# Paired units of a split-precision matmul kernel: the high and the low products in alternation instead of one run after the other

## What is computed

```python
def reference(x, ...):
    x = first_block(x, ...)      # norm, stick-breaking attention (16 heads), w_o, squared-ReLU MLP of width 8192
    return second_block(x, ...)  # 16 meta tokens ahead; w_in (12288 wide), pooling and conv branches, gates,
                                 # conv_out_w, w_o, gated MLP of width 5632 (w_gate_up, w_down), final norm
```

## Time and profile before

| | |
|---|---|
| median of 3 runs | 2644.3 us |
| the profiled execution, its own time | 2644.36 us |
| its span, first to last instruction | 2642.6 us |
| outside of the span | 1.8 us |
| TensorE matmul busy | 2620.2 us (99%), 16669 matmuls |
| VectorE / ScalarE / GpSimd busy | 63% / 46% / 15% |
| DMA | 54.7% of the 16 engines' time, 183 GB/s |
| highs (L1154) | 5248, of 512 columns |
| lows (L1160) | 5248, of 256 columns |

### The profile page before, as it was taken

The page is one execution under the profiler, slowest core; times in us unless marked ns, Lnnn a source line. Parts: engine busy times, 40 slices in busy tenths (PEclk is TensorE's granted clock), DMA queues, the critical chain, the costliest instruction groups (busy, mean ns, idle before and its releaser), DMA issues.

```text
span 2642.6 us, 41760 instructions
## 1 busy us (share of the span) xinstructions
PE 2620.2 (99%) x16669; PEld 2375.9 (90%) x16669; DVE 1657.6 (63%) x1279; ACT 1204.7 (46%) x1161; POOL 396.9 (15%) x180
## 2 busy tenths in 40 slices
PE   8999999999999999999999999999999999999998
PEld 8999999888888888899899988888888888888898
DVE  5566666656556556898754776566756555655555
ACT  5455554444444444533533344444444444444444
POOL 2122222100001001442200530011211001100110
PEclk9999999999999999999999999999999999999999
DMA  7554455555555555554555555555555555555552
GB/s 233 186 174 149 157 176 185 184 189 190 191 188 184 186 190 191 175 181 166 204 183 185 181 190 185 184 189 191 185 186 187 191 191 188 183 186 190 191 190 97
DMA packets 242948, 484.25 MB, mean 183 GB/s; under 512 B 7600, under 2 KB 7808, under 8 KB 242816
## 3 DMA queue, kind: packets, MB, share of 16 engines
q1 hardware_dynamic: 242800, 482.60, 54.7%
q10 hardware_dynamic: 32, 0.01, 0.0%
HBM read 480.49 MB, written 2.10 MB: 183 GB/s over the span
## 4 chain that ended last, share of the span: by engine, by line
PE 94%; issue 3%; POOL 1%; DVE 1%; ACT 1%; DMA 0%; ACTq 0%; POOLq 0%; DVEq 0%
PE ps L1154 44%; PE ps L1160 22%; PE ps L1172 15%; PE ps L1178 7%; PE ps L1142 2%; PE ps L1148 1%; POOL S L982 1%; POOL U L1023 0%; POOL a_buf L977 0%; DVE wlo L680 0%; PE ps L1121 0%; PE ps L1122 0%; PE ps L1120 0%; PE ps L1227 0%; PE ps L1204 0%
## 5 line engine op out<-in xcount | busy, mean ns | idle before, releaser
L680 DVE TENSOR_TENSOR wlo<-raw,whi 128x1024 fp32r<-128x1024 f32 x912 | 1263.2, 1398 | 929.1 <-ACT whi L511 928.6
L511 ACT ACTIVATE whi<-raw 128x1024 fp32r<-128x1024 f32 x912 | 964.6, 1060 | 1324.6 <-PE ps L1160 990.5
L1154 PE MATMUL ps<-b_buf,whi 128*128 128x512 f32 x2688 | 673.3, 392 | 0.0
L1154 PE MATMUL ps<-a_buf,whi 128*128 128x512 f32 x2560 | 645.7, 394 | 0.0
L1154 PEld LDWEIGHTS ps<-b_buf,whi 128*128 128x128 f32 x2688 | 483.5, 189 | 86.5
L1154 PEld LDWEIGHTS ps<-a_buf,whi 128*128 128x128 f32 x2560 | 459.7, 188 | 84.8
L1160 PEld LDWEIGHTS ps<-b_buf,wlo 128*128 128x128 f32 x2688 | 366.7, 190 | 26.2
L1172 PE MATMUL ps<-a_buf,whi 128*128 128x256 f32 (+4 forms) x2944 | 382.0, 282 | 2.5 <-POOL a_buf L954 2.5
L1160 PE MATMUL ps<-b_buf,wlo 128*128 128x256 f32 x2688 | 374.8, 282 | 0.0
L1160 PEld LDWEIGHTS ps<-a_buf,wlo 128*128 128x128 f32 x2560 | 346.9, 188 | 27.1
L1172 PEld LDWEIGHTS ps<-a_buf,whi 128*128 128x128 f32 x2944 | 364.0, 189 | 3.7 <-POOL a_buf L954 3.3
(11 more groups left out here) (181 smaller groups left out, 1110.0 us busy)
## 6 DMA issues: line engine op xcount, KB each, us to landing
raw<-in_mlp_w_dram SPq DMA_DIRECT2D x128, 1024.0 KB, 5.2
raw<-in_w_in_dram SPq DMA_DIRECT2D x96, 1024.0 KB, 5.0
raw<-in_w_gate_up_dram SPq DMA_DIRECT2D x88, 1024.0 KB, 4.8
raw<-in_sb_w_qkv_dram SPq DMA_DIRECT2D x48, 1024.0 KB, 5.2
raw<-in_w_down_dram SPq DMA_DIRECT2D x44, 1024.0 KB, 5.1
raw<-in_sb_w_o_dram SPq DMA_DIRECT2D x16, 1024.0 KB, 5.2
raw<-in_conv_out_w_dram SPq DMA_DIRECT2D x16, 1024.0 KB, 5.1
raw<-in_w_o_dram SPq DMA_DIRECT2D x16, 1024.0 KB, 5.1
```

The costliest lines, as they stand in the source:

```text
L511: act.activation(whi[:, unit_of(n, u)], raw[:, n % RAW, u * UK:(u + 1) * UK, :], ACT.Copy).then_inc(w_hi, 1)
L680: dve.tensor_tensor(wlo[:, s], raw[:, n % RAW, u * UK:(u + 1) * UK, :], cast(whi[:, s]), ALU.subtract).then_inc(w_lo, 1)
L1154: pe.matmul(ps[:, 4 * half + j, :].rearrange("p (a n) -> p a n", a=2), whi[:, s, kt, j * P:(j + 1) * P], buf[:, :, x, tok], start=first an ...
```

## The change

In paired units the wait for `w_lo` moves ahead of the first high. Then, over the eight pairs of k-tile and output tile, the order is: high 0, then high 1, low 0, high 2, low 1, ... high 7, low 6, and at the end low 7. The matmuls themselves, their operands and their number stay as they are. `start=` stays on the highs of the first k-tile, `w_used` on the last low. Nothing changes in other kinds of units or on other engines.

```diff
                     elif p.kind in PAIRED:
                         tok = slice(off, off + T)
-                        for kt, x in kts:
-                            for j in range(JT):
-                                pe.matmul(ps[:, 4 * half + j, :].rearrange("p (a n) -> p a n", a=2),
-                                          whi[:, s, kt, j * P:(j + 1) * P], buf[:, :, x, tok],
-                                          start=first and kt == 0, stop=False, skip_group_check=True)
                         pe.wait_ge(w_lo, cnt.at("chunk") * UNITS + (u + 1))
-                        for kt, x in kts:
-                            for j in range(JT):
-                                last = pe.matmul(ps[:, 4 * half + j, T:2 * T], wlo[:, s, kt, j * P:(j + 1) * P],
-                                                 hi[:, x, tok], start=False, stop=stop and kt == UK - 1,
-                                                 skip_group_check=True)
+
+                        def high(kt, x, j):
+
+                            pe.matmul(ps[:, 4 * half + j, :].rearrange("p (a n) -> p a n", a=2),
+                                      whi[:, s, kt, j * P:(j + 1) * P], buf[:, :, x, tok],
+                                      start=first and kt == 0, stop=False, skip_group_check=True)
+
+                        def low(kt, x, j):
+
+                            return pe.matmul(ps[:, 4 * half + j, T:2 * T], wlo[:, s, kt, j * P:(j + 1) * P],
+                                             hi[:, x, tok], start=False, stop=stop and kt == UK - 1,
+                                             skip_group_check=True)
+
+                        order = [(kt, x, j) for kt, x in kts for j in range(JT)]
+                        high(*order[0])
+                        for at, back in zip(order[1:], order):
+                            high(*at)
+                            low(*back)
+                        last = low(*order[-1])
```

## The result

The changed kernel takes 2650.12 us (median of 14 runs, 2649.61 to 2650.36) against 2644.36 (14 runs): 5.8 us more, a ratio of 1.0022 with a 95% interval of 1.0015 to 1.0028. The forecast was 2631. The profiled execution took 2650.15 us, its span is 2648.4 (2642.6 before).

The account below looks back on a forecast made before the run. TensorE was taken as the bound, through the distance between matmul starts. Reordering -14.2 us and the earlier wait +0.5 sum to -13.7 us, from 2644.3 to 2630.6, say 2631, with an 8 in 10 range of 2598 to 2664.

Parts of the forecast that it names:

- The bound: TensorE's chain: highs 44% and lows 22% of the span, full clock, limited by the distance between matmul starts.
- The price of a pair, 0.347 us: One high plus one low in the alternating order, against 0.3494 (`b_buf`) and 0.3500 (`a_buf`) before.
- The term of -14.2 us: Gain on TensorE's chain from reordering: 6.5 us in pairs from `b_buf`, 7.7 us in those from `a_buf`.
- The edges' 0.113 and 0.228: In the old `b_buf` unit: a low behind a high 0.113 us, a high with a low next 0.228.
- Carrying `b_buf` over to `a_buf`: Edge prices read in `b_buf` units were applied to `a_buf` units, whose run as a whole is within 0.001.
- its own sign: The prediction called itself wrong if the pair came out at or above 0.3495 us, or under 0.344.
- The slow rival: In alternated units each size keeps its long value, low 0.120 and high 0.233: pair 0.353, kernel 2662 us; chance 0.25.
- The fast rival: In alternated units loads hide under highs: pair 0.341 us, 45.6 us less, kernel 2599; chance 0.15.
- The rival in which order doesn't matter: Uneven pace in units is independent of neighbours: pair 0.349 to 0.350, only the wait counts, 2645 us; chance 0.20.
- The banks: Neighbouring matmuls in one PSUM bank: none shared one before either, and sharing seems free; priced at nothing.
- The wait: Wait for `w_lo` eight highs earlier: one stretch near 1251 us costs +0.5 us; elsewhere the split's lead is positive.
- The range: 8 in 10 range for the kernel's time, from the fast case to the slow one: 2598 to 2664 us.

Follow-up runs that it names:

- e11: The kernel before the change with `b_buf` begun 64 bytes later, nothing else: 2630.94 us, ratio 0.9950.
- e2: The new alternating order only in paired units that read `a_buf`, the old order in those from `b_buf`: 2641.84 us, ratio 0.9990 to the kernel before.
- e3: The new alternating order only in paired units that read `b_buf`, the old order in those from `a_buf`: 2652.17 us, ratio 1.0030 to the kernel before.
- e4: The changed kernel without the lag, each low directly behind its own high on the same bank: 2654.49 us, ratio 1.0038 to the kernel before.
- e10: The changed kernel with each low two tiles behind instead of one, no neighbours sharing a bank: 2647.74 us, ratio 1.0013 to the kernel before.
- e1: The kernel before, old order, with only the wait for `w_lo` moved ahead of the first high: 2645.09 us, ratio 1.0002.
- e9: The kernel before with alternation in units from `a_buf` only and `b_buf` begun 64 bytes later: 2628.92 us, ratio 0.9943.

## Why the prediction was wrong, point by point

- **The bound** was right: the two lines carry the chain, the clock is full, and the loss lies between starts. That all of it stays in the time was nearly right: 0.7 us fell to the wait for GpSimd near 1151 us.
- **The price of a pair, 0.347 us, is the step that failed.** It was taken from the two edges of the unit from `b_buf` and carried over to `a_buf`. Measured: 2.82 / 8 = 0.3525 in `b_buf` units, 0.349 in `a_buf` units. The term of -14.2 us came out as +6.5. The edges' 0.113 and 0.228 weren't prices of a neighbour: e11 has lows at 0.114 in the middle of a run, with a low on each side, just by another start of `b_buf`. And in the changed kernel's `b_buf` units, where the neighbours are those that were priced, highs take from 0.224 to 0.241. Their mean is 0.235, above the 0.233 that was to be the worst; lows have 0.117, near what was taken. So it was the highs that cost. What I read as "a low behind a high is short" was one place in a sequence that repeats itself for that layout. The warning stood in the rows: the earlier trace rows show the same order at two paces, and I used the difference only as a correction.
- **Carrying `b_buf` over to `a_buf`** failed with it: the two moved in opposite directions (e2, e3). The prediction is wrong by its own sign (a pair of 0.3495 or more) for `b_buf`, and not for `a_buf`.
- **The slow rival** (0.353, chance 0.25) named the right size for `b_buf` (0.3525), but that was luck. Its sum was a low of 0.120 and a high of 0.233, where 0.117 and 0.235 came, and its mechanism, a load that barely fits beneath a low, isn't borne out: e11's lows hold their load in 0.114. And it would have hit `a_buf` too. The fast rival rests on the same idea, that lows in a run are at 0.120 because of their loads, and falls by the same row. (Its estimate of 2517 for a pair of 0.325 us comes to 2515 by the rows; nothing rests on it.)
- **The rival in which order doesn't matter** (2645, chance 0.20) was right that an uneven pace isn't the neighbour's doing, and wrong that an order then moves nothing: by buffer and layout it is worth from -7.5 to +47 ns a unit.
- **The banks** priced at nothing: e4 shows 16 ns more per `a_buf` unit, 2 ns a pair, and the lag by itself moved units by as much (e10). The change's stated aim was met before it, as said.
- **The wait**: +0.5 us forecast in one stretch near 1251 us. The size was right, 0.6 us in the trace and 0.7 in e1, whose interval holds 0. But there are two places, near 1244 and 1253, where a load waits 0.26 us each; "elsewhere the lead is positive" was not so at the first.
- **The range** ended at 2598 and 2664 and held the result, by the slow case, whose reasons failed; the direction, to which 0.53 was given, was wrong. 0.26 stood for slower. A price read from the edges of one pattern deserved a chance near even for either sign.

What stays open: by what path weights and stream meet, and a rule that says which distance is good. The load of the next matmul's weights runs during the stream of this one, and both read SBUF; that the two reads get in each other's way would fit all runs, but it is only argued, as no run separates load from stream.

## What to carry to other kernels

Where TensorE is the bound and starts lie wider apart than the columns ask for (0.349 against 0.320 us here), compare the same loop on two buffers before touching its order: if their paces differ, the layout may be at work, and an order tried on one layout then says little of the next. Try shifts of the streamed buffer against the weights first. Here 64 bytes gave 0.5%, 32 gave nothing and 128 cost 0.2%, while the reordering gave 0.1% where it helped (e2) and cost 0.3% where it hurt (e3). The best version here, e9, has both: 2628.92 us, 15.4 under the kernel before and 21.2 under the changed one.

## What the runs showed of the hardware that was not expected

A sequence of matmuls with its loads has a pace that depends on the byte distance between the weights and the moving operand in SBUF: 2757, 2793, 2805 and 2811 ns for one and the same 16 matmuls from `b_buf`, at shifts of 64, 0, 32 and 128 bytes, and 2793 again when all operands move together. At shift 0 every unit takes this time to 2 ns, at shift 64 it is 2741 and 2773 in turn. What an order costs depends on it too: +26 ns at shift 0, +47 at shift 64. None of it is seen as idle time: matmuls are booked busy at 99% in each of these kernels.
